# Starting the output projections in the mixers' last turns, moving part of the first modulation to TensorE, and filling the norms' pauses with matmuls of constants

## The reference

```python
def fox_attention(h, w_in, b_f, w_out):
    ...
    return jnp.einsum('bsd,de->bse', out, w_out)

h = h + rmsnorm(mixed, norm_gains[layer, 1])
hn = rmsnorm(h, norm_gains[layer, 2])
h = h + rmsnorm(swiglu_ffn(hn, ffn_w_in[layer], ffn_w_out[layer]), norm_gains[layer, 3])
```

## Time and profile before

| | |
|---|---|
| median of three runs | 2726.39 us (2717.85 to 2727.79) |
| the profiled execution | 2726.55 us, span 2724.5 us |
| PE busy | 2311.6 us (85%) |
| PE weight load | 1801.5 us (66%) |
| DVE busy | 1441.8 us (53%) |
| ACT busy | 596.8 us (22%) |
| GpSimd busy | 1581.2 us (58%) |
| mean granted clock of PE | 0.914 |

### The profile page before, as it was taken

How to read it: one execution, slowest core, us unless ns; L and a number is a source line. 1 busy time by engine, 2 the same in 40 slices (tenths; PEclk the granted TensorE clock), 3 DMA queues, 4 the chain that set the end, 5 groups by cost and what they waited for, 6 DMA issues and landing times. The chain is left out here.

```text
span 2724.5 us, 29110 instructions
## 1 busy us (share of the span) xinstructions
PE 2311.6 (85%) x9818; PEld 1801.5 (66%) x9818; DVE 1441.8 (53%) x2027; ACT 596.8 (22%) x1040; POOL 1581.2 (58%) x731
## 2 busy tenths in 40 slices
PE   2747677767879999979998899999799988899997
PEld 1535455536658887856666688878577766688786
DVE  7797887968853331155443532211788884522202
ACT  1202112141022221033332311100333332311101
POOL 2454444534528777863332687778544443777774
PEclk6879788888889999989997999999899998999999
DMA  4211111214512222321110222223111111222232
GB/s 190 65 43 62 38 62 46 69 46 162 185 39 92 92 92 93 104 75 62 55 62 31 77 94 96 95 93 100 54 55 54 46 54 46 78 92 94 91 101 85
DMA packets 56485, 216.09 MB, mean 79 GB/s; under 512 B 6232, under 2 KB 6232, under 8 KB 53232
## 3 DMA queue, kind: packets, MB, share of 16 engines
q1 hardware_dynamic: 52992, 206.96, 22.4%
q10 hardware_dynamic: 3440, 8.44, 0.9%
HBM read 213.23 MB, written 2.15 MB: 79 GB/s over the span
## 5 line engine op out<-in xcount | busy, mean ns | idle before, releaser
L681 POOL TENSOR_TENSOR w_hi<-raw,ones 128x1024 fp32r<-128x1024 f32 x342 | 701.2, 2050 | 1056.4 <-DMA raw<-in_wstream 1056.3
L684 POOL TENSOR_TENSOR w_lo<-raw,w_hi 128x1024 fp32r<-128x1024 f32 x342 | 841.9, 2462 | 26.8
L302 PE MATMUL ps<-u_hi,w_hi 128*128 128x512 f32 x1848 | 764.5, 414 | 102.2 <-DVE ypad L1400 78.1
L302 PE MATMUL ps<-u_lo,w_hi 128*128 128x512 f32 x1848 | 743.6, 402 | 0.0
L302 PE MATMUL ps<-u_hi,w_lo 128*128 128x512 f32 x1848 | 742.6, 402 | 0.0
L302 PEld LDWEIGHTS ps<-u_hi,w_hi 128*128 128x128 f32 x1848 | 356.0, 193 | 192.5 <-issue 102.1
L302 PEld LDWEIGHTS ps<-u_hi,w_lo 128*128 128x128 f32 x1848 | 354.9, 192 | 87.7
L302 PEld LDWEIGHTS ps<-u_lo,w_hi 128*128 128x128 f32 x1848 | 355.9, 193 | 81.3 <-issue 3.0
L302 PE MATMUL ps<-f_hi,w_hi 128*128 128x512 f32 x528 | 210.8, 399 | 7.7 <-ACTq L84 7.7
L302 PE MATMUL ps<-f_lo,w_hi 128*128 128x512 f32 x528 | 210.5, 399 | 0.0
L302 PE MATMUL ps<-f_hi,w_lo 128*128 128x512 f32 x528 | 210.3, 398 | 0.0
(11 more groups left out here) (297 smaller groups left out, 2882.9 us busy)
## 6 DMA issues: line engine op xcount, KB each, us to landing
raw<-in_wstream SPq DMA_DIRECT2D x342, 512.0 KB, 3.3
ada_buf<-in_ada SPq DMA_DIRECT2D x16, 1024.0 KB, 4.8
ada_start<-in_ada SPq DMA_DIRECT2D x8, 1024.0 KB, 16.8
cbc<-decay_rows ACTq DMA_DIRECT2D x8, 512.0 KB, 3.7
x<-in_xT SPq DMA_DIRECT2D x1, 2048.0 KB, 7.8
bc<-gate_rows ACTq DMA_DIRECT2D x4, 512.0 KB, 5.0
out_T<-x ACTq DMA_DIRECT2D x8, 256.0 KB, 2.0
prm<-in_params SPq DMA_DIRECT2D x1, 357.5 KB, 3.0
```

Of the source, the lines that this page charges most:

```text
L302: last = nc.tensor.matmul(out, a, b, start=(start and k == 0 and i == 0), stop=(stop and k == nk - 1 and i == 2))
L681: g.tensor_tensor(w_hi[slot][:], raw[slot][:], ones[:, 0:1].to_broadcast([P, D]), ALU.mult).then_inc(chunk_hi, 1)
L684: g.tensor_tensor(w_lo[slot][:], raw[slot][:], w_hi[slot][:].bitcast(f32), ALU.subtract).then_inc(chunk_split, 1)
```

## The change

1. **First modulation.** DVE keeps pieces 1, 3 and 5 (`ada_start_dve`). For pieces 0, 2, 4, 6 and 7 PE multiplies the fp32 piece itself: the scalar column is the weight, one column wide, and the piece's 256 columns stream (`ada_start_pe`), which gives a row of 256 sums on one partition. ACT copies the row to SBUF (`ada_start_act`), and two small matmuls turn it into two columns (`ada_start_columns_pe`). PE does pieces 0, 2 and 4 between the sums of squares, 6 and 7 after them. PE's start also waits for the constant `levels` to be complete.
2. **Shifted norms.** The product of x, gain and inverse root lies in PSUM banks 6 and 3 instead of SBUF tiles, and the inverse root stays in bank 7.
3. **Matmuls of constants.** `keep_busy` issues fp32 matmuls of 512 columns of constants into bank 2, which nobody reads: six after the sum of each norm of kind "late", three after the second sum of norm 1.
4. **Projections.** `MixerOut` replaces `out_pe` for the two mixers. In the last turn, after a wait for the last head's tiles to have left banks 0 to 2, each hook from the third (attention) or fifth (recurrence) on is followed by one step of the projection: three matmuls of one of the first seven tiles of the first three output tiles, 63 matmuls in all. `finish` then adds the eighth tile to each and does the other five output tiles. The projection rotates over three banks instead of two, and no longer waits for ACT to open `og.act`.

```diff
+    def keep_busy(pe, count):
...
+        for _ in range(count):
+            nc.tensor.matmul(ps[2][:], mean_w[:], levels[:, 0:4, :].bitcast(f32), start=True, stop=True)
...
     def norm_pe(pe, N, og):
...
             N.pe1.did(nc.tensor.matmul(ps[5][:], mean_w[:], sq[(KT - 1) % 2][:], start=False, stop=True), "sum")
+            if N.pre == "late":
+                keep_busy(pe, 6)
         if N.pre == "shift":
...
                 N.pe2.did(nc.tensor.matmul(ps[7][:], mean_w[:], sq[n % 2][:], start=(n == 0), stop=(n == KT - 1)), "sum")
+            keep_busy(pe, 3)
...
                 N.asq.did(nc.scalar.activation(sq[n % 2][:], x[:, n, :], ACT.Square), "sq")
+                if not N.post and n in (3, 5, 7):
+                    ada_start_act(act, ADA_PE[n // 2 - 1])
             act.wait_ge(N.pe2.sem, N.pe2.at("sum", KT - 1))
-            inverse_root(act, N.a2, rms, ps[7], 1)
+            inverse_root(act, N.a2, ps[7], ps[7], 1)
+            if not N.post:
+                for p in ADA_PE[3:]:
+                    ada_start_act(act, p)
             for n in range(KT):
                 act.wait_ge(N.vt.sem, N.vt.at("t", n))
-                N.ah.did(nc.scalar.activation(u_hi[:, n, :], sq[n % 2][:], ACT.Identity, bias=shift(n)), "hi")
+                N.ah.did(nc.scalar.activation(u_hi[:, n, :], ps[(6, 3)[n % 2]][:], ACT.Identity, bias=shift(n)), "hi")
...
                 dve.wait_ge(N.ah.sem, N.ah.at("hi", n))
-                N.vl.did(nc.vector.scalar_tensor_tensor(u_lo[:, n, :], sq[n % 2][:], shift(n),
+                N.vl.did(nc.vector.scalar_tensor_tensor(u_lo[:, n, :], ps[(6, 3)[n % 2]][:], shift(n),
                                                         u_hi[:, n, :].bitcast(f32), ALU.add, ALU.subtract), "lo")
...
                     dve.wait_ge(N.vl.sem, N.vl.at("lo", n - 2))
-                N.vt.did(nc.vector.scalar_tensor_tensor(sq[n % 2][:], x[:, n, :], gain(n), rms[:],
+                N.vt.did(nc.vector.scalar_tensor_tensor(ps[(6, 3)[n % 2]][:], x[:, n, :], gain(n), ps[7][:],
                                                         ALU.mult, ALU.mult), "t")
...
-    def out_act(act, og, base, ks):
+    class MixerOut:
...
+        def __init__(self, og, base, hi, lo, ready):
+            self.og, self.base, self.hi, self.lo, self.ready = og, base, hi, lo, ready
+            self.todo = [(n, k) for n in range(GROUP) for k in range(KT - 1)]
...
+        def step(self, pe, n, k):
+            slot = (self.base + n) % SLOTS
+            wh, wl = w_hi[slot][:, k * P:(k + 1) * P], w_lo[slot][:, k * P:(k + 1) * P]
+            for i, (a, b) in enumerate(tri(wh, wl, self.hi(k), self.lo(k))):
+                last = nc.tensor.matmul(ps[n % GROUP][:], a, b, start=(k == 0 and i == 0), stop=(k == KT - 1 and i == 2))
+            return last
...
+        def fill(self, pe, count=1):
+            for _ in range(min(count, len(self.todo))):
+                n, k = self.todo.pop(0)
+                if k == 0:
+                    pe.wait_ge(chunk_split, self.base + n + 1)
+                if n == 0:
+                    pe.wait_ge(self.ready.sem, self.ready.at("lo", k + 1))
+                self.step(pe, n, k)
...
+        def finish(self, pe):
+            self.fill(pe, len(self.todo))
+            pe.wait_ge(self.ready.sem, self.ready.at("lo", KT))
+            for n in range(GROUP):
+                self.step(pe, n, KT - 1).then_inc(gemm_done, 1)
+            for n in range(GROUP, KT):
+                pe.wait_ge(self.og.act.sem, self.og.act.at("copy", n - GROUP))
+                pe.wait_ge(chunk_split, self.base + n + 1)
+                for k in range(KT):
+                    last = self.step(pe, n, k)
+                last.then_inc(gemm_done, 1)
...
+    def out_act(act, og, base, ks, banks=2):
         nch = len(ks)
...
                 act.wait_ge(og.dve.sem, og.dve.at(f"acc{max(n - 2, 1)}"))
-            og.act.did(nc.scalar.activation(sq[n % 2][:], ps[n % 2][:], ACT.Square), "sq")
-            og.act.did(nc.scalar.activation(m[:, n, :], ps[n % 2][:], ACT.Identity), "copy")
+            og.act.did(nc.scalar.activation(sq[n % 2][:], ps[n % banks][:], ACT.Square), "sq")
+            og.act.did(nc.scalar.activation(m[:, n, :], ps[n % banks][:], ACT.Identity), "copy")
...
-    def ada_dve_pieces(dve, turn, start=False):
+    def ada_dve_pieces(dve, turn):
         for s in range(ADA_BODY):
             b = s % 2
-            if start:
-                piece = ada_start[:, ADA_BODY * turn + s]
-                dve.wait_ge(ada_start_landed[ADA_BODY * turn + s], 16)
-            else:
-                piece = ada_buf[b]
-                dve.wait_ge(ada_landed[b], 32 * (turn - ADA_FIRST // ADA_BODY) + 16 * (s // 2) + 16)
+            piece = ada_buf[b]
+            dve.wait_ge(ada_landed[b], 32 * turn + 16 * (s // 2) + 16)
             for k in range(KT):
...
+    def ada_start_dve(dve):
...
+        for i, p in enumerate(ADA_DVE):
+            dve.wait_ge(ada_start_landed[p], 16)
+            for k in range(KT):
+                if k == 0:
+                    ins = nc.vector.tensor_scalar(ada_acc0[:, i, :], ada_start[:, p, 0, :], cvec[:, 0:1], None, ALU.mult)
+                else:
+                    dve.wait_ge(v_ada0.sem, v_ada0.at(f"l{p}_{k - 1}"))
+                    ins = nc.vector.scalar_tensor_tensor(ada_acc0[:, i, :], ada_start[:, p, k, :], cvec[:, k:k + 1],
+                                                         ada_acc0[:, i, :], ALU.mult, ALU.add)
+                v_ada0.did(ins, f"l{p}_{k}")
+        dve.wait_ge(p_ada0.sem, p_ada0.at("sums"))
+        v_ada0.did(nc.vector.tensor_tensor(mod[:, 0:2 * KT], ps[6][:, 0:2 * KT], prm[:, COL["ada_b"]:COL["ada_b"] + 2 * KT],
+                                           ALU.add), "mod")
...
+    def ada_start_pe(pe, p):
...
+        i = ADA_PE.index(p)
+        pe.wait_ge(ada_start_landed[p], 16)
+        for k in range(KT):
+            last = nc.tensor.matmul(ps[(0, 1, 2, 4, 5)[i]][0:1, 0:ADA_COLS], cvec[:, k:k + 1],
+                                    ada_start[:, p, k, :], start=(k == 0), stop=(k == KT - 1))
+        p_ada0.did(last, f"r{p}")
...
+    def ada_start_columns_pe(pe, p):
...
+        i = ADA_PE.index(p)
+        pe.wait_ge(a_ada0.sem, a_ada0.at(f"r{p}"))
+        for h in range(ADA_COLS // P):
+            j = p * (ADA_COLS // P) + h
+            last = nc.tensor.matmul(ps[6][:, j:j + 1], ada_row[0:1, i, h * P:(h + 1) * P], ones[0:1, 0:1],
+                                    start=True, stop=True)
+        return last
...
+    def ada_start_act(act, p):
+        i = ADA_PE.index(p)
+        act.wait_ge(p_ada0.sem, p_ada0.at(f"r{p}"))
+        a_ada0.did(nc.scalar.activation(ada_row[0:1, i, :], ps[(0, 1, 2, 4, 5)[i]][0:1, 0:ADA_COLS],
+                                        ACT.Identity), f"r{p}")
...
+    def ada_start_sums_pe(pe):
+        for i, p in enumerate(ADA_DVE):
+            pe.wait_ge(v_ada0.sem, v_ada0.at(f"l{p}_{KT - 1}"))
+            for h in range(ADA_COLS // P):
+                j = p * (ADA_COLS // P) + h
+                last = nc.tensor.matmul(ps[6][:, j:j + 1], ada_acc0[:, i, h * P:(h + 1) * P], ones[:, 0:1],
+                                        start=True, stop=True)
+        return last
...
     ada_link = Steps(ctx, nc, "ada_link", [f"l{s}{k}" for s in range(ADA_BODY) for k in range(KT - 1)])
...
         n = ADA_BODY * ADA_COLS // P
-        s_ada.did(nc.vector.tensor_tensor(mod[:, bass.ds(n * turn, n)], ps[6][:, 0:n],
-                                          prm[:, bass.ds(COL["ada_b"] + n * turn, n)], ALU.add), "mod")
+        s_ada.did(nc.vector.tensor_tensor(mod[:, bass.ds(2 * KT + n * turn, n)], ps[6][:, 0:n],
+                                          prm[:, bass.ds(COL["ada_b"] + 2 * KT + n * turn, n)], ALU.add), "mod")
...
         pe.wait_ge(const_ready, 14)
-        pe.wait_ge(v_set.sem, v_set.at("c"))
-        norm_pe(pe, norms[0], None)
-        for turn in range(ADA_FIRST // ADA_BODY):
-            ada_pe(pe, turn)
...
+        pe.wait_ge(v_set.sem, v_set.at("lv7"))
         N0 = norms[0]
+        for n in range(KT):
+            pe.wait_ge(N0.asq.sem, N0.asq.at("sq", n))
+            N0.pe2.did(nc.tensor.matmul(ps[7][:], mean_w[:], sq[n % 2][:], start=(n == 0), stop=(n == KT - 1)), "sum")
+            if n in (1, 3, 5):
+                ada_start_pe(pe, ADA_PE[n // 2])
+        for p in ADA_PE[:3]:
+            ada_start_columns_pe(pe, p)
+        ada_start_sums_pe(pe)
+        ada_start_pe(pe, ADA_PE[3])
+        ada_start_pe(pe, ADA_PE[4])
+        ada_start_columns_pe(pe, ADA_PE[3])
+        p_ada0.did(ada_start_columns_pe(pe, ADA_PE[4]), "sums")
...
         gemm_chunk(pe, C_GATE1, 0, ps[5][:], u_tiles, u_lows, 0, KT, True, True,
...
                ready=lambda k: pe.wait_ge(v_ln.sem, v_ln.at(f"hl{k}" if k < KT else f"lo{k - KT}")),
-               extra=lambda it: ada_pe(pe, ADA_FIRST // ADA_BODY + it))
+               extra=lambda it: ada_pe(pe, it))
...
             else:
```

(41 more changed lines are left out.)

## The result

The changed kernel takes 2677.47 us (median of four, 2674.21 to 2682.19) against 2726.04 for the kernel before (2717.85 to 2727.79): ratio 0.983, 95% interval 0.9815 to 0.9845. Its profiled execution took 2677.04 us (span 2675.0). The forecast was 2679, so the total is right. Its terms are not all right, and part of the agreement is chance, as the stretches show.

A forecast was written before the change was run, and what follows sets the result against it. DVE bounds the first modulation and the first mixer until 640 us, then PE's matmuls set the end. Terms -20.5 - 12 - 8 - 7.5 = -48 from 2726.6 give 2679 us; own range 2668 to 2692, 8 in 10 2662 to 2703.

The forecast's parts named there:

- Part 1: First modulation: PE takes five of DVE's eight pieces, so normalised x begins at 44 us instead of 64.7, -20.5.
- Rival A: First modulation: PE's row products run at the low clock, the start gains nothing, 2699 us; chance 0.13.
- The move to PSUM: Norm under GpSimd's first four splits: intermediate moved from SBUF costed at nothing, +6 us if DVE were blocked all the same.
- Part 2: Attention mixer: 63 projection matmuls go into the last turn, net -12 us, bounds -14 and -6.
- The projection's term: Attention projection behind the last turn: 32.5 us including two waits instead of 44.9, so -12.4.
- the added wait ... +0.9: Attention's last turn: waiting for the last head's value tile holds weighing, rounding and ACT's next exponent, +0.9 us.
- in return PE's own work runs at full clock: Attention's last turn: full clock instead of 0.52 for most of it, last weighing 2.0 us instead of 4.0, -2.
- Part 3: Gated recurrence's last turn and projection: fills lengthen level gaps, +6.1 us, projection saves 13.4; net -8, bounds -11 and +5.
- Part 4: Norms: constants' matmuls fill PE's pauses and avoid cold starts, -1.4 us in each of four, -2 in another, together -7.5.
- B: Mixers: fills hold turns up more, or GpSimd's splits delay the next norm; gain 8 us instead of 20, 2691; chance 0.15.
- C: Norms: constants' matmuls do nothing, since the last 1.6 us of idleness lowers the clock, 2686 us; chance 0.1.
- D: Whole kernel slower: light, broken work never earns 2.4 GHz, start gains 0, fills and constants cost; +31, 2757 us; chance 0.02.

## Why the prediction was right, and where it was not

**Part 1 holds in mechanism and size.** Forecast -20.5, shown by the old start under the rest -21.3. PE's stage ended at 41.15 us against 42.3, with two terms off in opposite ways: the sixteen small matmuls took 4.1 us (1.49 and 1.50 for six each, 1.13 for four), not 7.1, for their price of 0.44 came from a stretch at the low clock; the five pieces took 18.3 (3.97, twice 3.61, 7.07 for two), not 17.1. Rival A falls by the clock of 1.00. A piece's work lasted 3.6 us, and PE did not stand idle for the next. The rule of the Trainium skill, TensorE: Matmul & The Clock Gate, "HAM oscillation", speaks of work shorter than the wait for the next; that case did not occur, and the trace agrees with it so far. The move to PSUM costs nothing, as said, and without it the norm ends 3.6 us later.

**Part 2 fails at the turn.** The projection's term is right (-11.8 against -12.4, with both waits at their places, 1.41 and 1.14). The turn was to grow by 0.4 and grew by 4.0, from 34.7 to 38.7 us. The step that failed is "the added wait ... +0.9" together with "in return PE's own work runs at full clock": the wait is 1.4, and the weighing and the first fills behind it run at half clock, another 4.0, most of which goes when the wait is moved or filled. The full clock came only 10 us later. The forecast gave the fills credit for the clock and did not ask whether a new wait takes it away.

**Part 3 is mis-sized at the levels.** Mechanism as forecast (level starts 3.0 us apart, the first gap 5.7, the off-diagonal products 0.8 earlier). The gap was priced at 2.9 and 4.8, in sum 22.2 us; it came to 23.9. The projection behind it began, at 2243.26, 8.0 us later against the first level than before (forecast 6.3) and then ran 32.5 us, where 32.0 was forecast without its 1.1 of waiting. That makes -5.8 in this trace (-6.0 by the means) for -8.

**Part 4 holds** in mechanism, and its size is known only within a few us. Against the forecast of -7.5, the table's two traces put 6.5 on norms 2 to 5 (some 0.7 of it is the projections' earlier tile in norms 3 and 5) and 2.7 on norm 1, 9.2 in all. The trace without the constants lost 5.5 in the five norms. The 8.8 of its median can't be split and may hold the pauses ahead of the down projections.

**The sum** was right by errors that cancel, as far as the stretches show. The mixers gave 14.0 instead of 20, the start gave 1 us more, and some 5 us came by chance: 3.6 from two pauses ahead of the down projections, 1.3 from the first mixer. The parts as the stretches measure them (21.5, 8.0, 6.0, and 5.5 to 9.2 for the constants) make 41 to 45 us of the 49.5. The medians tell it otherwise. Taking out the start, the fills and the constants costs 21.3, 18.6 and 8.8 us there, 48.7 in sum, which is close to the forecast's own terms. Each of these three has some 7 us to either side, and a stretch repeats much better, so the account above follows the stretches. Which part of the medians' difference, 48.6, is chance was not settled.

**The rivals.** B named the right place, but its price of 12 us was about twice what was lost, and its second half did not occur: GpSimd split the next phase's third chunk by 1496.29, and the norm's first tile came at 1498.88. C and D are out.

## What to carry to other kernels

Work put into an engine's idle gaps should go where the engine waits longest for something that is not behind it (ahead of the chain, behind the chain), not into the gaps of the chain itself: spreading 21 groups that way more than doubled this edit's gain in the recurrence (5.8 to 13.4 us). A wait added ahead of a turn costs its length and can cost the cold matmuls behind it, so put each wait at the first instruction that needs it, and price the clock at every new pause. Filling a pause with matmuls of constants pays only where PE sets the pace; ask first who waits next.

## What was not expected of the hardware

- The same pause of 2.11 us ahead of the down projections was followed by the low clock in 11 of 20 cases and not in 9, 1.5 us each; with two matmuls of constants in it, in none of four. Even the 3.43 us ahead of the first down projection were followed by full clock in three of twelve traces. With six such places in the attention's turns (pauses of 0.95 and 1.31 us) that stretch scattered over 7 us between kernels with the same code; with constants in the pause it took 250.4 and 250.3 us. The Trainium skill, TensorE: Matmul & The Clock Gate, "What's actually happening", says of a kernel's first matmuls that how many are cold varies from run to run; here the same holds for pauses in the middle.
- A one-column fp32 matmul that turns 128 numbers of a row into a column took 0.24 to 0.28 us at full clock (six in 1.49, four in 1.13), and eight fp32 products of a 1-column weight with 256 columns 3.6 us at clock 1.00.
- DVE's 128x256 product with both inputs in SBUF took 0.42 us alone and 1.92 to 2.59 under a split of GpSimd. In the twelve traces none of the 1155 such instructions without a GpSimd instruction beside it took over 0.46 us.
